# A two-block transformer kernel on one core: another order of weight splits, evacuations and residuals

## The reference, cut to what matters

```
block 1:  h = rms_norm(x);  proj = h @ w_in                       # 1024 x 8708
          four kinds of attention on slices of proj (stick-breaking, dilated, forgetting, differential)
          x = x + sum(sigmoid(gates) * (branches @ w_branch)) @ w_out
          h = rms_norm(x);  x = x + square(relu(h @ w_up)) @ w_down   # 4096 hidden
          x = rms_norm(x)                                         # final norm
block 2:  h = rms_norm(x);  q, k, v, u = split(h @ w_in_2)
          attn = causal attention of 8 heads on rope(rms_norm(q)), rope(rms_norm(k)), v
          conv = silu(layer_norm(depthwise_conv31(glu(u))))
          x = x + concat(attn, conv) @ w_out_2
          h = rms_norm(x);  x = x + (silu(h @ w_gate) * (h @ w_up)) @ w_down   # 2816 hidden
```

## Time and profile before

| what | value |
|---|---|
| median of three runs | 852.4 us (852.08 to 854.29) |
| the profiled execution: own time | 851.74 us |
| its span in the trace | 849.9 us |
| TensorE busy | 808.7 us, 95% of the span |
| VectorE, ScalarE, GpSimd busy | 467.8, 418.9, 33.9 us |
| mean granted TensorE clock | 0.992 |
| weights read | 134.4 MB, 159 GB/s over the span |

### The profile page before, as it was taken

How to read it: one execution, slowest core, us unless ns; L and a number is a source line. 1 busy time by engine, 2 the same in 40 slices (tenths; PEclk the granted TensorE clock), 3 DMA queues, 4 the chain that set the end, 5 groups by cost and what they waited for, 6 DMA issues and landing times.

```text
span 849.9 us, 9710 instructions
## 1 busy us (share of the span) xinstructions
PE 808.7 (95%) x3930; PEld 664.5 (78%) x3930; DVE 467.8 (55%) x616; ACT 418.9 (49%) x549; POOL 33.9 (4%) x33
## 2 busy tenths in 40 slices
PE   6998999999999998999999998999988999999997
PEld 5876888877778777788888876877876788888896
DVE  6443444556766776454444437689745555444543
ACT  6576455445555735545444436555436443344341
POOL 0000000000000310000000003021000000000000
PEclk9999999999999999999999999999989999999999
DMA  9742323443455444655555555744102754654441
GB/s 345 273 140 84 125 84 123 141 148 108 142 172 174 149 164 168 197 198 189 175 177 179 180 171 198 267 152 153 51 6 98 244 170 142 233 197 149 131 167 50
DMA packets 68268, 136.25 MB, mean 160 GB/s; under 512 B 2304, under 2 KB 7040, under 8 KB 67584
## 3 DMA queue, kind: packets, MB, share of 16 engines
q1 hardware_dynamic: 67760, 134.44, 46.9%
q10 hardware_dynamic: 464, 1.20, 0.4%
HBM read 134.43 MB, written 1.05 MB: 159 GB/s over the span
## 4 chain that ended last, share of the span: by engine, by line
PE 84%; DVE 7%; ACT 5%; issue 2%; POOL 1%; DMA 0%; ACTq 0%; DVEq 0%; SPq 0%
PE b L536 18%; PE b L538 18%; PE b L537 18%; PE SS L536 4%; PE SS L538 4%; PE SS L537 4%; PE TT L505 4%; DVE wlo L1401 2%; PE OO L536 2%; PE OO L538 2%; PE OO L537 2%; PE OO L845 2%; PE SS L621 1%; ACT whi L998 1%; PE b L680 1%
## 5 line engine op out<-in xcount | busy, mean ns | idle before, releaser
L1401 DVE TENSOR_TENSOR wlo<-raw,whi 128x2048 fp32r<-128x2048 f32 (+2 forms) x123 | 271.8, 2218 | 104.9 <-ACT whi L998 104.9
L998 ACT CAST whi<-raw 128x2048 fp32r<-128x2048 f32 (+2 forms) x123 | 227.6, 1850 | 123.6 <-PE b L538 92.3
L536 PE MATMUL b<-whi,Ahi 128*128 128x512 f32 (+2 forms) x568 | 223.0, 393 | 10.2 <-DVE wlo L1401 3.7
L538 PE MATMUL b<-whi,Alo 128*128 128x512 f32 (+2 forms) x568 | 216.5, 381 | 0.0
L537 PE MATMUL b<-wlo,Ahi 128*128 128x512 f32 (+2 forms) x568 | 216.3, 381 | 0.0
L536 PEld LDWEIGHTS b<-whi,Ahi 128*128 128x128 f32 x568 | 108.2, 190 | 34.0 <-issue 8.1
L538 PEld LDWEIGHTS b<-whi,Alo 128*128 128x128 f32 x568 | 107.9, 190 | 21.0
L537 PEld LDWEIGHTS b<-wlo,Ahi 128*128 128x128 f32 x568 | 108.3, 191 | 18.5
L536 PE MATMUL b<-whi,Bhi 128*128 128x512 f32 x168 | 66.7, 397 | 5.5 <-DVE wlo L1401 2.8
L1415 DVE TENSOR_TENSOR hlo<-TT,hhi 128x512 fp32r<-128x512 f32 (+1 forms) x28 | 17.7, 668 | 91.3 <-ACT hhi L1012 91.3
L538 PE MATMUL b<-whi,Blo 128*128 128x512 f32 x168 | 65.5, 390 | 0.0
(11 more groups left out here) (269 smaller groups left out, 1011.6 us busy)
## 6 DMA issues: line engine op xcount, KB each, us to landing
raw<-in_w_in SPq DMA_DIRECT2D x42, 1024.0 KB, 5.1
raw<-in_w_up SPq DMA_DIRECT2D x16, 1024.0 KB, 5.4
raw<-in_w_dn SPq DMA_DIRECT2D x16, 1024.0 KB, 7.3
raw<-in_w_d SPq DMA_DIRECT2D x11, 1024.0 KB, 5.1
raw<-in_w_g SPq DMA_DIRECT2D x10, 1024.0 KB, 5.3
raw<-in_w_u SPq DMA_DIRECT2D x10, 1024.0 KB, 5.0
raw<-in_w_out SPq DMA_DIRECT2D x8, 1024.0 KB, 5.0
raw<-in_w_br SPq DMA_DIRECT2D x4, 1024.0 KB, 5.0
```

The source lines that it names most:

```text
L536: e.matmul(dst, xh, H[:, kc, c0:ce], start=first and kc == krs[0], stop=False)
L538: ins = e.matmul(dst, xl, H[:, kc, c0:ce], start=False, stop=last and kc == krs[-1])
L998: e.copy(whi[:, s, 0:m], raw[:, r, 0:m]).then_inc(s_hi, 1)
L1401: e.tensor_tensor(wlo[:, s, 0:m], raw[:, r, 0:m], whi[:, s, 0:m].bitcast(F32), ALU.subtract).then_inc(s_lo, 1)
```

## The change

1. **Splits.** `split_after` takes the place of `ends`: unit i is cast at the group `free_at[i-3]`, the first group after its slot has been read for the last time, and VectorE subtracts at the group after that. In `PLAIN` order that is one group earlier than before.
2. **Order within a group.** Evacuations, residuals and norm work come before `after` or `before` in p1, p2, up, dn, g, u and the output projections; in p1 and p2 the stage work stays behind. The order in the branch products (br), and VectorE's order in p1 and p2 (`before`, then stage work), are not edited.
3. **Groups.** `FIRST` remains for the first chunk of p1 alone. The output projections and the last down product run by column halves; quarters are completed, squared, turned and gained in the order ORD = (0,0), (1,0), (0,1), (1,1) in (t, n). Evacuations of token half 0 in the first chunks of up, p2 and g move from the third to the fourth group.
4. **Banks.** p2 accumulates in banks 1 and 2, `ap` writes bank 0.
5. **Timetable.** The first transposition of the GLU gate half (`gt` 0) moves from stage 2 to 3, its sigmoid (`gs` 0) from 3 to 4.
6. **Convolution.** Heads 4 to 7 have one part of the convolution, not two; the four others go to the last two rounds, behind the last `ap`, and behind the transpositions of the attention output.

```diff
+ORD = [(0, 0), (1, 0), (0, 1), (1, 1)]
...
-    bg[2] += [("gt", 0)]
-    bg[3] += [("gs", 0)]
-    bg[4] += [("gt", 1)]
+    bg[3] += [("gt", 0)]
+    bg[4] += [("gs", 0), ("gt", 1)]
...
-        for t in range(2):
-            for n in range(2):
-                group(u[1][n], name, 1, n, t)
+        for n, t in PLAIN:
+            group(u[1][n], name, 1, n, t)
...
-    ends = {}
     for tag, i in unit_of.items():
         free_at[i] = groups[tag] + 1
-    for i, g in free_at.items():
-        ends[g - 1] = i
+    split_after = {}
+    for i in range(NPC, nu):
+        g = free_at[i - NSPL] if i >= NSPL else 0
+        assert g not in split_after, (g, i)
+        split_after[g] = i
...
-                    clear(t)
+                    clear(1 + t)
...
-                product(("p2", i, ui, t), Ahi, Alo, 4 * ui, t, lambda c0, t=t: bank[t], ui == 0, ui == 1)
+                product(("p2", i, ui, t), Ahi, Alo, 4 * ui, t, lambda c0, t=t: bank[1 + t], ui == 0, ui == 1)
...
+        def tile_part():
+            conv(n_conv[0])
+            n_conv[0] += 1
+
         for k in range(10):
             if k < 8:
                 az(k)
-                conv(2 * k)
+                tile_part()
             if 1 <= k < 9:
                 at(k - 1)
-            if k < 8:
-                conv(2 * k + 1)
+            if k < 4 or k > 7:
+                tile_part()
             if k > 1:
                 ap(k - 2)
+        tile_part()
         for t in range(2):
             key = ("Y", t, 0)
             xbank[key] = next_t()
             w.wait_ge(s_aw, 8)
             turn_x(key, ys[:, t, 0:512])
+        tile_part()
...
         def after(*tag):
-            i = ends.get(groups[tag])
-            if i is not None and i + 2 < nu:
-                split_hi(i + 2)
+            if groups[tag] in split_after:
+                split_hi(split_after[groups[tag]])
...
             for q, (ui, t) in enumerate(order1(c)):
-                after("p1", c, ui, t)
                 if q == 0 and c:
                     evac(c - 1, 1)
                 if q == (2 if c == 0 else 3):
                     evac(c, 0)
+                after("p1", c, ui, t)
                 stages1(4 * c + q)
...
-                if q == (2 if j == 0 else 3):
+                after("up", j, ui, t)
+                if q == 3:
                     relu2(j, 0)
...
-                if q == (2 if i == 0 else 3):
+                if q == 3:
                     evac2(i, 0)
+                after("p2", i, ui, t)
                 stages2(4 * i + q)
...
+        split_done = [0]
         def before(*tag):
-            i = ends.get(groups[tag] - 1)
-            if i is not None and i + 2 < nu:
-                split_lo(i + 2)
+            i = split_after.get(groups[tag] - 1)
+            if i is not None and i > split_done[0]:
+                split_lo(i)
+                split_done[0] = i
...
-            for t in range(2):
-                for n in range(2):
-                    before(name, 1, n, t)
-                    w.wait_ge(s_mm, done(name, 1, n, t))
-                    residual(base, t, n)
-                    if (t, n) != (0, 0):
-                        p = ((0, 0), (0, 1), (1, 0))[2 * t + n - 1]
-                        gained((norm, *p), pcol(gain, 4 * p[1], 4))
+            for k, (t, n) in enumerate(ORD):
+                w.wait_ge(s_mm, done(name, 1, n, t))
+                residual(base, t, n)
+                if k:
+                    p = ORD[k - 1]
+                    gained((norm, *p), pcol(gain, 4 * p[1], 4))
+                before(name, 1, n, t)
```

More of the change, by code:

```diff
@@ L325, in plan_down, with plan_up @@
                 group(u, name, j, 0, t)
-    def plan_up(name, src, j, n, first):
+    def plan_up(name, src, j, n):
         u = [add_unit(src, 4 * k, 4, 512 * j, n) for k in range(2)]
-        for ui, t in (FIRST if first else PLAIN):
+        for ui, t in PLAIN:
             group(u[ui], name, j, ui, t)
@@ L772, in _, with up @@
                         turn_x(("M", t_, 1), ys[:, t_, 512:1024])
-        for t in range(2):
-            for n in range(2):
-                bk = W_ACC[t, n]
-                w.wait_ge(s_xl, X["M", t, 1] + 1)
-                product(("wo", 1, n, t), Ahi, Alo, 4, t, lambda c0, bk=bk: bank[bk], False, True)
-                gone[bk] = (s_res, 2 * t + n + 1)
-                if (t, n) != (0, 0):
-                    turn_res("N1", *((0, 0), (0, 1), (1, 0))[2 * t + n - 1])
-        def up(name, j, src, hi, lo, first, tail=None):
-            for q, (ui, t) in enumerate(FIRST if first else PLAIN):
+        for k, (t, n) in enumerate(ORD):
+            bk = W_ACC[t, n]
+            w.wait_ge(s_xl, X["M", t, 1] + 1)
+            product(("wo", 1, n, t), Ahi, Alo, 4, t, lambda c0, bk=bk: bank[bk], False, True)
+            gone[bk] = (s_res, k + 1)
+            if k:
+                turn_res("N1", *ORD[k - 1])
+        def up(name, j, src, hi, lo, tail=None):
+            for q, (ui, t) in enumerate(PLAIN):
                 bk = 1 + t
@@ L794, in down @@
             hi, lo = hhi[:, j % 2], hlo[:, j % 2]
-            for k, (n, t) in enumerate([(n, t) for t in range(2) for n in range(2)] if last else PLAIN):
+            for k, (n, t) in enumerate(PLAIN):
                 bk = W_ACC[t, n]
@@ L1175, in out_proj @@
                         ln_silu()
-            for t in range(2):
-                for n in range(2):
-                    after(name, 1, n, t)
-                    if (t, n) != (0, 0):
-                        p = ((0, 0), (0, 1), (1, 0))[2 * t + n - 1]
-                        norm_turn(norm, *p, o)
-                        gained((norm, *p))
+            for k, (t, n) in enumerate(ORD):
+                if k:
+                    norm_turn(norm, *ORD[k - 1], o)
+                    gained((norm, *ORD[k - 1]))
+                after(name, 1, n, t)
         out_proj("wo", "N1", o2)
-        def plain_order(first):
-            return FIRST if first else PLAIN
         def relu2(j, t):
@@ L1358, in _ @@
         for j in range(6):
-            for q, (ui, t) in enumerate(plain_order(j == 0)):
-                after("g", j, ui, t)
+            for q, (ui, t) in enumerate(PLAIN):
                 if j == 0 and q == 0:
@@ L1713, in _ @@
         for j in range(8):
-            for q, (ui, t) in enumerate(FIRST if j == 0 else PLAIN):
+            for q, (ui, t) in enumerate(PLAIN):
                 before("up", j, ui, t)
@@ L1732, in _ @@
         w.wait_ge(s_sq, SQ["N1", 1, 1] + 1)
-        for k, (t, n) in enumerate(PLAIN):
-            before("dn", 7, n, t)
+        for k, (t, n) in enumerate(ORD):
             w.wait_ge(s_mm, done("dn", 7, n, t))
@@ L1861, in _ @@
         for i in range(5):
-            for q, (ui, t) in enumerate(FIRST if i == 0 else PLAIN):
+            for q, (ui, t) in enumerate(PLAIN):
                 before("p2", i, ui, t)
@@ L1892, in ln @@
                                 ALU.mult).then_inc(s_lv, 1)
-        ends.pop(groups["wo2", 0, 0, 0] - 1, None)
         w.wait_ge(s_dve, k_x)
```

136 lines of the change are left out of this document (65 added, 71 removed).

## The result

The changed kernel takes **856.4 us** (median of four runs, 856.26 to 856.62), the kernel before 852.2 in the same comparison: ratio 1.0044, 95% interval 1.0026 to 1.0061. That is 0.4% slower, where 0.5% faster was forecast, and outside the range. The profiled execution took 856.35 us with a span of 854.5, against 849.9 before, so the two traces differ by 4.6 us.

A forecast was written before the change was run, and what follows sets the result against it. TensorE, busy 95% of the span, was taken as the bound, so only its waits and slow clock could change. Terms summed to -4.2 us, 847.5 from the profiled 851.7; with medians 0.7 higher, 848.0 us, range 841.5 to 853.5.

The forecast's parts named there:

- Pair copies: First input projection, stages 29 and 37: subtractions ahead of the query and key pair copies delay them, +5.2 us together.
- two such losses of 1.6: +3.2: First input projection: half clock after each of the two longer pair-copy waits, +3.2 us, bounds 0 and +5.
- TensorE waits for softmax work in stages 30 to 40: First input projection: a sign named beforehand that would show the forecast wrong.
- Rival 3: First input projection: VectorE's subtraction also delays two further dilated tiles, each 2.5 + 1.6; 856 us, chance 0.10.
- my walk gives +1.1: Branch products: a 1.5 us evacuation wait, one gated-product wait going and one of some 2.5 arising; bounds -1.0 and +4.
- Output projection into the MLP: Into the first MLP chunk: earlier splits remove 2.8 us of waits, later ReLU work becomes the limit; -2.3 us.
- Second output projection: Around it: split waits at its units and gate chunk and the slow clock after attention go; -7.0 us.
- MLP into the second projection: Start of the second input projection: residual wait and slow clock go, first evacuation no earlier; one group gained, -2.7 us.
- its interior: Inside the second input projection: subtractions before the rotary work delay key pairs, +1.3 us, bounds 0 and +3.
- rival 1: First input projection: pair copies cost little or the clock holds; -8 to -12 us, 842 us, chance 0.20.
- Rival 2: Three further idle stretches each bring half clock, +1.6 each; 852.5 us, no change, chance 0.20.
- Rival 4: Splits start no earlier, so waits of 2.8 + 2.7 us for them remain; 853.5 us, chance 0.04.

The follow-up runs named there:

- experiment 1: The changed kernel, but in stages 29 and 37 of the first input projection VectorE does its stage work before the subtraction: 845.2 us, ratio 0.9927.
- experiment 6: The changed kernel with 24 extra short TensorE products ahead of the waiting transposition in stages 28 and 36: 848.9 us, ratio 0.9961.
- experiment 2: As experiment 1, with VectorE's stage work ahead of the subtraction in stage 39 too: 844.6 us, ratio 0.9913.
- experiment 3: The changed kernel with the first input projection's casts and subtractions in their old places: 840.8 us, ratio 0.9877.
- experiment 4: As experiment 3, with the branch products' splits in their old places too: 838.6 us, ratio 0.984.
- experiment 10: As experiment 4, but in stage 17 of the second input projection VectorE scales the third rotary tile before its subtraction: 836.0 us, ratio 0.9817.
- experiment 7: As experiment 4, but with the convolution parts distributed over the heads as in the kernel before: 845.1 us, ratio 0.9898.
- experiment 8: As experiment 4, but in the second input projection's first chunk ScalarE evacuates token half 0 ahead of the second weight cast: 841.3 us, ratio 0.9856.
- experiment 5: The changed kernel, but at the first branch product ScalarE does the projection's last evacuation and a sigmoid ahead of the cast: 856.2 us, ratio 1.0056.

## Why the prediction was wrong

It forecast -4.2 us, the traces give +4.6. The difference of 8.8 is made up of 4.0 in the first input projection, 4.0 in the branch products, 1.1 in the second projection, 1.2 in the attention, less 1.6 where it did better or the run began earlier (8.7 with rounding).

**Pair copies, forecast +5.2:** right. 7.2 for 2.1 is +5.1, by the mechanism named, and experiment 1 takes it back. "If the cast were done before the head's product" did not arise.

**Clock there, "two such losses of 1.6: +3.2":** this term failed by size, 2.5 + 3.1 = 5.6. The price was taken from the earlier trace rows, where the half clock followed an idle time of 2.4 us in 2.95; behind 3.5 and 3.7 us with nothing busy it lasted over 6 us. The earlier trace rows held the longer case too: clock 0.53 for 5.0 us behind the attention, which the prediction itself priced at 2.2 for another term. Its upper bound of +5 was too low as well. Experiment 6 shows that idleness sets it.

**"TensorE waits for softmax work in stages 30 to 40"** was named as what would make the forecast wrong, and it came, once: +1.4. Rival 3 wanted two tiles for its 856 us. The time came out near it, but one tile was caught (experiment 2), at no clock, and most of the rest came from the two other terms. So rival 3 had the right place and engine, and not the right sum.

**Branch products, "my walk gives +1.1":** this step failed, +5.1, beyond its own bound of +4. The evacuation was right (1.4). That "one of the waits of 1.3 to 1.4 goes" for the one that arises was not: gated products cost 1.5 us more in waits than before and the half clock behind the last one another 1.6, which experiment 3, with the same waits at full clock, does not have (+3.5 for +5.1). The sum was off on its own terms too: 1.5 for the evacuation, less 1.4 for the wait that goes, plus 2.5 for the one that arises, is +2.6 and not +1.1. Experiment 4 takes all of it back by moving only splits. The fault of method is that one engine was walked exactly and the other in words: from "an odd place earlier" follows that two or three subtractions stand ahead of gated products that had none ahead before.

**Output projection into the MLP, -2.3:** right, -2.9. **Second output projection, -7.0:** right, -7.7, with the waits of the earlier trace rows gone and a clock of 1.00 throughout 632 to 643 us.

**MLP into the second projection, -2.7, and its interior, +1.3:** half right. The first group starts 2.7 earlier; the residual's wait is gone. The evacuation's wait was forecast at 2.9 and was 2.1. Not forecast was the wait for a split (1.7), which had no place in the working at all. By group 176 of the list nearly all is paid back: -0.3 for -1.4. But 1.6 of that is the half clock behind the evacuation (window 546.2), which had no place in the forecast; experiment 4, with the same waits and full clock there, keeps -1.8. The subtraction ahead of the third rotary tile was named, and measured at 2.7 in waits; it is part of the -1.8 of the attention, whose -3.0 would otherwise have been passed: experiment 10, without that wait, has -3.9 there, and experiment 7 gives the convolution's part as 3.2 in the attention and 1.4 behind it, near the -3.0 and -2.2 forecast. (Two sums here are off by 0.2: 3.8 less 0.6 is 3.2, and 847.5 plus 0.7 is 848.2.)

**On the rivals:** rival 1 is refuted, as the copies were late and the clock fell. Rival 2, that each new idle stretch brings half clock, was wrong as a rule but right on one of its three: the stretch before the first evacuation brought it (window 546.2), the 2.7 us before the third rotary tile did not (window 595.3), and the one at the MLP's first chunk did not arise. It priced the right quantity, at 1.6 each. The Trainium skill, "TensorE: Matmul & The Clock Gate", "Why this matters for your kernels", advises against gaps of TensorE between bursts of products; the runs bear this out more strongly than the forecast did, at 5.6 us for two of them. Rival 4 is refuted: no wait for splits is left between 280 and 345 us.

The chance of 0.66 for faster went with a sum of eight terms. The three of the first half, +9.5 forecast, came to +17.5; the five behind them, -13.7 forecast, came to -12.7. The faster kernel was in the change; its first half hid it.

## What to carry to other kernels

Work that can be issued earlier may be issued earlier only up to the first engine whose queue it then heads: ask of every moved instruction what is due next behind it, and leave the moved order alone in stages where nothing had waited for it. Price a wait of the bound engine with the slow clock it can bring, which here was as much as the wait itself. When a change of several parts comes out at nothing, put each part back by itself: +17 and -13 us may lie side by side.

## What was not expected of the hardware

**After short idleness the clock falls in some runs and holds in others.** The same instructions with the same waits were granted different clocks in different kernels. These windows show the 2.1 us wait for the first evacuation of the second projection and the products behind it, first in experiment 4, then in experiment 7, whose code up to there is the same:

```profile
527.00:529.50 2.50, 0.40 (x3) 0.05 (x1) 2.43 (x3) 2.50 (x4) 0.23 (x1) 1.00 1.01 419
529.50:533.30 3.80, 3.80 (x21) 3.25 (x22) 3.80 (x3) 3.29 (x6) 0.00 (x0) 1.00 1.01 418
```

```profile
527.00:529.50 2.50, 0.40 (x3) 0.30 (x3) 2.48 (x3) 2.50 (x3) 0.00 (x0) 0.98 1.01 416
529.50:533.30 3.80, 3.80 (x13) 3.13 (x12) 3.80 (x2) 3.04 (x6) 0.00 (x0) 0.56 0.99 407
```

The wait of 2.2 us for a gated product was followed by 0.64 over 4.7 us in the changed kernel and in experiment 1, by 1.00 in experiments 3 and 6. The wait of 2.7 us for the third rotary tile kept full clock behind it in the changed kernel and in experiments 3, 6, 7 and 8, and had half clock behind it in experiments 1, 2, 4 and 5. Even the ordinary wait of 1.07 us for the first pair copy, followed by full clock in experiments 1 and 3, had this behind it in experiment 2:

```profile
118.00:124.00 6.00, 6.00 (x42) 5.98 (x40) 4.75 (x5) 3.50 (x5) 0.00 (x0) 0.74 0.28 76
```

There the fall came 1.9 us after the end of the wait, so it is not shown that this wait brought it. Only behind waits of 3.5 us and more was it always there, four times in the two profiled runs that had them (the changed kernel and experiment 5). The Trainium skill, "TensorE: Matmul & The Clock Gate", Part 1, calls the number of products that run at the slow clock at a kernel's start variable from run to run; these windows show the same in the middle of a kernel. What decides in the short cases was not found here; each such place spreads the group starts by 1.6 us between profiled runs, and single runs of one kernel here differ by up to 4.8 us (experiment 6, 847.9 to 852.8).

**A subtraction that starts beside GpSimd waits for it.** Where the second projection begins, VectorE's and GpSimd's work on large tiles overlaps (changed kernel, first VectorE, then GpSimd):

```profile
534.89 3.38 DVE L1401 TENSOR_TENSOR wlo<-raw,whi 128x2048 fp32r<-128x2048 f32 x1
```

```profile
524.47 1.30 POOL L1970 TENSOR_TENSOR xr<-xr,par 128x512 f32<-128x512 f32 x1 [170.81 <-PE TT L507]
527.65 2.25 POOL L1970 TENSOR_TENSOR xr<-xr,par 128x512 f32<-128x512 f32 x1 [1.89 <-PE TT L507]
533.13 2.99 POOL L1970 TENSOR_TENSOR xr<-xr,par 128x512 f32<-128x512 f32 x2 [3.22 <-ACT ys L1155]
```

The subtraction takes 3.38 us where it takes 2.28 elsewhere, and one gain multiplication on GpSimd 2.25 where it takes 1.30 with VectorE less in its way. GpSimd ends at 536.12; from there to the end of the subtraction at 538.27 it is 2.15 us, about its usual length, so it reads as if VectorE had stood still until GpSimd was done. The Trainium skill, "SBUF — State Buffer", Who interferes with whom, says that a VectorE instruction with two inputs in SBUF, as this one has, contends with a GpSimd instruction that reads SBUF, and that the lock on the ports they share is exclusive. The trace agrees, within 0.15 us. The split that TensorE waits 1.7 us for is this one, so some 1.1 of them may come from GpSimd; moving its work was not tried.
